# Second norm taken half by half of the tokens, in a one-core two-layer decoder step

## The reference, cut to what matters

```python
h = rmsnorm(x, norm_w) * (1 + scale) + shift      # scale, shift, gate from the condition
y = (mixer(h @ w_in) * silu(z)) @ w_out
x = x + gate * y
```

## Time and profile before

| what | before |
|---|---|
| median of three runs | 1167.5 us |
| profiled execution, its own time | 1165.51 us |
| its span | 1163.8 us |
| TensorE matmuls busy | 1124.7 us (97%) |
| VectorE busy | 627.2 us (54%) |
| ScalarE busy | 506.7 us (44%) |
| GpSimd busy | 150.7 us (13%) |
| mean granted TensorE clock | 0.989 |

### The profile page before, as it was taken

One profiled execution on the slowest core, in us unless ns is written; L12 is line 12 of the kernel. 1 busy time (PEld: TensorE's weight loads), 2 busy tenths in 40 slices (PEclk: granted clock), 3 DMA queues, 4 the chain that ended last, 5 costly groups with the idle time before them and its releaser, 6 DMA issues.

```text
span 1163.8 us, 25951 instructions
## 1 busy us (share of the span) xinstructions
PE 1124.7 (97%) x11029; PEld 1050.7 (90%) x11029; DVE 627.2 (54%) x1241; ACT 506.7 (44%) x1026; POOL 150.7 (13%) x156
## 2 busy tenths in 40 slices
PE   8999999999999999989998999999999999999998
PEld 6898988988898889869997999999999999998997
DVE  4766575667566666674333743453365336436432
ACT  4643344444444444453112544554365255447121
POOL 1000000101010101000000450162035005400000
PEclk9999999999999999989999999999999999999999
DMA  9863525352535343516233437432832562252531
GB/s 325 280 181 112 160 64 167 95 168 83 151 109 158 103 150 110 156 55 189 73 88 121 113 101 152 120 87 81 197 86 82 121 168 62 76 140 67 173 100 54
DMA packets 232153, 147.71 MB, mean 127 GB/s; under 512 B 7811, under 2 KB 226141, under 8 KB 231526
## 3 DMA queue, kind: packets, MB, share of 16 engines
q1 hardware_dynamic: 217392, 134.17, 40.3%
q10 hardware_dynamic: 14646, 11.89, 3.0%
HBM read 124.00 MB, written 22.02 MB: 125 GB/s over the span
## 4 chain that ended last, share of the span: by engine, by line
PE 86%; DVE 6%; issue 2%; ACT 2%; DMA 2%; SPq 1%; DVEq 0%; ACTq 0%
PE PJ L380 25%; PE PJ L1556 17%; PE PJ L1271 14%; PE PJ L401 7%; PE X L1153 1%; PE X L1249 1%; PE X L1672 1%; PE X L1167 1%; PE PJ L1581 1%; PE PJ L427 1%; PE X L1637 1%; PE X L1699 1%; PE PJ L624 1%; PE X L1120 1%; PE X L1251 1%
## 5 line engine op out<-in xcount | busy, mean ns | idle before, releaser
L353 DVE TENSOR_TENSOR w_lo<-raw,w_hi 128x1024 fp32r<-128x1024 f32 (+1 forms) x128 | 156.8, 1238 | 173.1 <-ACT w_hi L345 172.4
L345 ACT ACTIVATE w_hi<-raw 128x1024 fp32r<-128x1024 f32 (+1 forms) x128 | 129.1, 1024 | 156.8 <-PE PJ L1556 73.1
L1556 PE MATMUL PJ<-w_hi,h_hi 128*128 128x256 f32 x600 | 167.5, 287 | 0.8 <-DVE w_lo L353 0.7
L1556 PE MATMUL PJ<-w_lo,h_hi 128*128 128x256 f32 x600 | 164.6, 283 | 0.0
L380 PE MATMUL PJ<-h_hi,w_hi 128*128 128x288 f32 (+1 forms) x736 | 161.5, 301 | 0.2 <-ACT v_ L870 0.2
L380 PE MATMUL PJ<-h_hi,w_lo 128*128 128x288 f32 (+1 forms) x736 | 157.7, 296 | 0.0
L380 PE MATMUL PJ<-h_lo,w_hi 128*128 128x288 f32 (+1 forms) x736 | 157.3, 295 | 0.0
L1556 PE MATMUL PJ<-w_hi,h_lo 128*128 128x256 f32 x480 | 135.8, 283 | 0.0
L380 PEld LDWEIGHTS PJ<-h_hi,w_hi 128*128 128x128 f32 x736 | 118.1, 189 | 4.7 <-issue 3.8
L380 PEld LDWEIGHTS PJ<-h_hi,w_lo 128*128 128x128 f32 x736 | 118.9, 189 | 0.0
L380 PEld LDWEIGHTS PJ<-h_lo,w_hi 128*128 128x128 f32 x736 | 118.8, 189 | 0.0
(11 more groups left out here) (323 smaller groups left out, 2176.3 us busy)
## 6 DMA issues: line engine op xcount, KB each, us to landing
raw<-in_a_w_in_dram SPq DMA_DIRECT2D x48, 512.0 KB, 4.1
raw<-in_ada_w_dram SPq DMA_DIRECT2D x32, 512.0 KB, 3.7
raw<-in_b_w_in_dram SPq DMA_DIRECT2D x64, 256.0 KB, 3.4
kvc<-in_cache_kv_w_dram SPq DMA_DIRECT2D x24, 512.0 KB, 5.9
pre<-in_ada_w_dram SPq DMA_DIRECT2D x16, 512.0 KB, 10.0
s<-in_state_hgrn_dram SPq DMA_DIRECT2D x8, 1024.0 KB, 6.7
out_hgrn_sample_dram<-s ACTq DMA_DIRECT2D x8, 1024.0 KB, 5.0
raw<-in_a_w_out_dram SPq DMA_DIRECT2D x16, 512.0 KB, 5.1
```

Source lines behind the costliest of these rows:

```text
L345: act.activation(w_hi[:, i % SPLITS, 0:size], raw[:, n % RAWS, 0:size], ACT.Copy).then_inc(hi_done, 1)
L353: dve.tensor_tensor(w_lo[:, i % SPLITS, 0:size], raw[:, n % RAWS, 0:size], w_hi[:, i % SPLITS, 0:size].bitcast(F32), ALU.subtract).then_in ...
L1556: last = pe.matmul(PJ[:, tile // 2, tile % 2 * 256:tile % 2 * 256 + 256], a, b[:, k, :], start=(first and k == 0 and i == 0), stop=(kk == ...
```

## The change

**TensorE.** Output block 7 is made in two passes instead of one (`pe_out_halves`). Pass e takes, of every four consecutive tokens, the two with r = 2e and 2e+1: 288 tokens per matmul, read from the operand in strided pairs, and written side by side in one PSUM bank. Each pass walks all 16 input blocks. `norm_pe` of block 6 stands between the passes; block 7's sum of squares is made by halves, the first within pass 1, the second within the first attention rows.

**The norm.** All of it is done for the prompt tokens of half 0 (256 of them) and then of half 1. The squares are now written in turned order, by two ScalarE instructions per block. The samples go with half 1, and their four VectorE instructions or parts of such are now on GpSimd (`second_norm_seqs`).

**The first rows.** Tiles 0 and 1 are made for all feature blocks, then tiles 2 and 3.

```diff
 def norm_pe(sq, k):
-            for e in range(2):
-                last = pe.matmul(X[:, e, 0:HT], ones[:], sq[:, k % 2, e * HT:(e + 1) * HT],
-                                 start=(k == 0), stop=(k == KD - 1))
+            for e, (n0, n1) in enumerate(((0, HP), (HP, T))):
+                last = pe.matmul(X[:, e, 0:n1 - n0], ones[:], sq[:, k % 2, n0:n1], start=(k == 0), stop=False)
...
+        def norm_pe_last(sq, e):
+            pe.wait_ge(n_sq, 2 * KD + e)
+            n0, n1 = ((0, HP), (HP, T))[e]
+            pe.matmul(X[:, e, 0:n1 - n0], ones[:], sq[:, (KD - 1) % 2, n0:n1], start=False, stop=True).then_inc(n_ms, 1)
 def norm_square(xT, sq, k):
-            act.activation(sq[:, k % 2, :], xT[:, k, :], ACT.Square).then_inc(n_sq, 1)
+            act.activation(quarters(sq[:, k % 2, 0:TP]), perm(xT[:, k, 0:TP]), ACT.Square)
+            act.activation(sq[:, k % 2, TP:T], xT[:, k, TP:T], ACT.Square).then_inc(n_sq, 1)
 def second_norm_act(act, chain):
+            def inverse_root(e):
+                n0, n1 = ((0, HP), (HP, T))[e]
+                act.wait_ge(n_ms, 5 + KD + e)
+                chain(act.activation(rn1[:, n0:n1], X[:, e, 0:n1 - n0], ACT.Ln, bias=eps[:, 0:1], scale=1.0 / D))
+                act.activation(rnp[:, n0:n1], rn1[:, n0:n1], ACT.Exp, scale=-0.5).then_inc(n_r, 1)
...
+            last_square(0)
+            inverse_root(0)
+            act.wait_ge(out_half, 2)
+            hi(0, 0, 2)
+            split_hi(("a", 0, 1))
+            hi(0, 2, 5)
+            last_square(1)
+            hi(0, 5, KD)
+            inverse_root(1)
+            hi(1, 0, 5)
+            act.wait_ge(n_hs, 4)
+            act.activation(h_hi[:, :, TP:T], xa[:, :, TP:T], ACT.Copy).then_inc(n_hs, 1)
+            hi(1, 5, KD)
             split_hi(("a", 0, 2))
+        def second_norm_dve(dve, chain):
...
+            residual_half(chain, 0)
+            amplify_half(0)
             dve.wait_ge(n_xs, KD)
             dve.wait_ge(n_r, 2)
+            scale_x(0, 0)
             for k in range(1, KD):
+                scale_x(0, k)
+                low(0, k - 1)
                 if k == 2:
                     split_lo(("a", 0, 1))
+                if k == 4:
+                    residual_half(chain, 1)
+                    amplify_half(1)
+            dve.wait_ge(n_xs, KD + 1)
+            dve.wait_ge(n_r, 3)
+            scale_x(1, 0)
+            low(0, KD - 1)
+            for k in range(1, KD):
+                scale_x(1, k)
+                low(1, k - 1)
+            low(1, KD - 1)
             split_lo(("a", 0, 2))
+        def second_norm_seqs(pool):
+            xs = xa[:, :, TP:T]
+            pool.wait_ge(n_xs, KD + 1)
+            pool.wait_ge(n_r, 3)
+            nc.gpsimd.tensor_tensor(xs, xs, rnp[:, TP:T].unsqueeze(1).to_broadcast([P, KD, TS]), ALU.mult).then_inc(n_hs, 1)
+            pool.wait_ge(n_hs, 3)
...
+            nc.gpsimd.tensor_tensor(by_seq, by_seq, ada[:, 1, 0:KD, 1:].unsqueeze(3).to_broadcast([P, KD, DB, DS]),
+                                    ALU.add).then_inc(n_hs, 1)
+            pool.wait_ge(n_hs, 5)
+            for low_seqs in (h_hi[:, :, T:T + TS], h_lo[:, :, TP:T]):
+                nc.gpsimd.tensor_tensor(low_seqs, xs, h_hi[:, :, TP:T].bitcast(F32), ALU.subtract).then_inc(n_hs, 1)
+        def pe_out_halves(pe):
+            m = KD - 1
+            t = begin(OUT0 + m)
+            for e in range(2):
+                for n in range(16):
+                    if n % 8 == 0:
+                        pe.wait_ge(raw_split, split_no[("out0", m, n // 8)][0] + 1)
+                    wh, wl = parts_of(("out0", m, n // 8))
+                    for i, (a, b) in enumerate(((wh, o_hi(n)), (wh, oz_low[:, n, :]), (wl, o_hi(n)))):
+                        last = pe.matmul(PJ[:, 2 * t + e, 0:HT].rearrange("p (a r) -> p a r", r=2), a[:, n % 8, :],
+                                         b.rearrange("p (a r) -> p a r", r=4)[:, :, 2 * e:2 * e + 2],
+                                         start=(n == 0 and i == 0), stop=(n == 15 and i == 2))
+                    if n == 15 if e == 0 else 7 <= n < 15:
+                        last.then_inc(out_half, 1)
+                    if e == 1 and n == 4:
+                        norm_pe_last(nsq1, 0)
+                if e == 0:
+                    norm_pe(nsq1, m - 1)
+            last.then_inc(pj_ready, 1)
 def pe_first_rows(pe):
+            for e in range(2):
+                for k in range(KD):
+                    if e == 0 and k % 4 == 0:
+                        pe.wait_ge(raw_split, split_no[("a", 0, k // 4)][0] + 1)
+                    if e == 1 and k == 0:
+                        wait_read(pe, OUT0 + KD - 1)
+                    pe.wait_ge(n_hx, KD * (1 + e) + k + 1)
+                    pe.wait_ge(n_lo, KD * (1 + e) + k + 1)
+                    for tile in (2 * e, 2 * e + 1):
+                        last = product(PJ[:, tile, 0:256], tile, k)
+                    if e == 0 and k == 4:
+                        norm_pe_last(nsq1, 1)
+                last.then_inc((tiles_ready, pj_ready)[e], 1)
+            pe.wait_ge(n_hs, 6)
```

More of the change, by code:

```diff
@@ L218, in program @@
         n_hx = sem("n_hx")
+        out_half, x_half = sem("out_half"), sem("x_half")
         par_in, par_t, par_done = sem("par_in"), sem("par_t"), sem("par_done")
@@ L518, in amplify @@
             dve = nc.vector
-            seqs = lambda ap: ap.rearrange("p (b t) -> p b t", b=DB)
             wait_read(dve, OUT0 + m)
             dve.tensor_scalar(quarters(xa[:, m, 0:TP]), perm(xT1[:, m, 0:TP]), amp[:, m, 0:1], None, ALU.mult)
[L522 to L533, removed]
+            amplify_seqs(m)
@@ new lines, in amplify_seqs, with amplify_half @@
+        def amplify_seqs(m):
+            seqs = lambda ap: ap.rearrange("p (b t) -> p b t", b=DB)
+            nc.vector.tensor_tensor(seqs(xa[:, m, TP:T]), seqs(xT1[:, m, TP:T]),
+                                    amp[:, m, 1:].unsqueeze(2).to_broadcast([P, DB, DS]), ALU.mult).then_inc(n_xs, 1)
+        def amplify_half(e):
+            dve, m, r = nc.vector, KD - 1, slice(2 * e, 2 * e + 2)
+            if e == 0:
+                dve.wait_ge(x_half, 1)
+            else:
+                wait_read(dve, OUT0 + m)
+            ins = dve.tensor_scalar(quarters(xa[:, m, 0:TP])[:, r], perm(xT1[:, m, 0:TP])[:, r], amp[:, m, 0:1], None, ALU.mult)
+            if e == 0:
+                ins.then_inc(n_xs, 1)
+            else:
+                amplify_seqs(m)
@@ new lines, in residual_half @@
+        def residual_half(chain, e):
+            dve, m = nc.vector, KD - 1
+            s = m % 2
+            if e == 0:
+                dve.wait_ge(out_half, 1)
+            else:
+                dve.wait_ge(pj_ready, OUT0 + m + 1)
+            fours = lambda ap: ap.rearrange("p (a r) -> p a r", r=4)[:, :, 2 * e:2 * e + 2]
+            y = PJ[:, 2 * s + e, 0:HT].rearrange("p (a r) -> p a r", r=2)
+            x = fours(xT1[:, m, 0:TP])
+            dve.scalar_tensor_tensor(out=x, in0=y[:, 0:P], scalar=ada[:, 0, 2 * KD + m, 0:1], in1=x,
+                                     op0=ALU.mult, op1=ALU.add).then_inc(x_half, 1)
+            by_seq = lambda ap: ap.rearrange("p (b a) r -> p b a r", b=DB)
+            chain(dve.tensor_tensor(by_seq(fours(yg[:, s])), by_seq(y[:, P:]),
+                                    ada[:, 0, 2 * KD + m, 1:].unsqueeze(2).unsqueeze(3).to_broadcast([P, DB, 2, 2]), ALU.mult))
+            if e:
+                dve.tensor_tensor(xT1[:, m, TP:T], xT1[:, m, TP:T], yg[:, s], ALU.add).then_inc(pj_read[s], 1)
@@ new lines, in second_norm_dve, with scale_x, low @@
+        def second_norm_dve(dve, chain):
+            def scale_x(e, k):
+                c = slice(HP * e, HP * e + HP)
+                dve.tensor_tensor(xa[:, k, c], xa[:, k, c], rnp[:, c], ALU.mult).then_inc(n_xr, 1)
+            def low(e, k):
+                c = slice(HP * e, HP * e + HP)
+                dve.wait_ge(n_hx, KD * (1 + e) + k + 1)
+                if e == 0 and k < KD - 1:
+                    dve.wait_ge(out_half, 3 + k)
+                dve.scalar_tensor_tensor(out=h_lo[:, k, c], in0=xa[:, k, c], scalar=ada[:, 1, k, 0:1],
+                                         in1=h_hi[:, k, c].bitcast(F32), op0=ALU.add, op1=ALU.subtract).then_inc(n_lo, 1)
+            residual_half(chain, 0)
+            amplify_half(0)
@@ L2508, in _ @@
                     split_lo(("a", 0, 0))
-                dve_residual(dve, chain, 0, OUT0 + m, m, xT1, yg)
-                amplify(m)
+                if m < KD - 1:
+                    dve_residual(dve, chain, 0, OUT0 + m, m, xT1, yg)
+                    amplify(m)
                 if m == 3:
                     attention_tables(dve, chain)
-            second_norm_dve(dve)
+            second_norm_dve(dve, chain)
             attention_masks(dve)
@@ L2540, in _ @@
             pe.wait_ge(ada_done, 4 + AH)
-            for m in range(1, KD):
+            for m in range(1, KD - 1):
                 pe_out(pe, "out0", m, range(16))
```

(2 more changed lines are left out.)

74 lines of the change are left out of this document (31 added, 43 removed).

## The result

| what | before | after |
|---|---|---|
| median of five runs | 1166.64 us | 1174.74 us |
| lowest and highest | 1165.81 to 1167.86 | 1171.14 to 1176.68 |
| profiled execution, its own time | 1165.51 us | 1174.44 us |
| its span | 1163.8 us | 1172.8 us |
| TensorE matmuls busy | 1124.7 us (97%) | 1136.8 us (97%) |

The ratio is 1.0064, with a 95% interval of 1.0051 to 1.0077: slower by 7.5 us (8.1 us between the medians), and outside the range of the prediction. Note the two rows that an engineer would look at first. TensorE's share and its mean clock have hardly moved, and both look healthy. What the table hides is that TensorE's busy time got 12.1 us longer for the same multiplications.

A forecast was written before the change was run, and what follows sets the result against it. TensorE, busy 97%, was taken as the bound, with VectorE taking the path after the change. Pass 0, its wait and the rest, 6.4 + 0.9 + 31.1 = 38.4 us against 38.7, gave a median of 1167.2 us, range 1163.0 to 1170.5.

The forecast's parts named there:

- The step that failed: Block 7's two passes: strided-pair matmuls cost nothing extra, 6.4 us for 48; the other end was 6.4 more per pass.
- the sum of 38.4: Forecast from block 7's start to TensorE's second weight piece: 6.4 + 0.9 + 31.1 us, against 38.7 before.
- the stretch: From the norm matmuls' end ahead of block 7 to TensorE's start on the next head group's second weight piece, 38.70 us before.
- Rival C: Block 7's passes: TensorE reads pairs at half the rate, 10.1 us more together, 1177.3 us; chance 0.12.
- the first inverse root: Half 0's norm on ScalarE: done at E+4.4 us, E being the end of pass 0; logarithm and exponential about 0.5 each.
- rival B: Half 1 of the norm: GpSimd costs VectorE nothing, 4.4 us come back, 1162.8 us; chance 0.24.
- Pass 0 and its wait: Block 7's first pass: 6.4 us of matmuls plus a 0.9 us wait for a low part of the output weights.
- forecast A: The main forecast: TensorE's gap and slow clock go, VectorE takes the path, 0.3 us faster, 1167.2 us; chance 0.50.
- VectorE's pitches: VectorE in half 0 of the norm: 0.34 us per scale_x and 0.40 per low part.
- GpSimd against VectorE: Half 1 of the norm: each of four GpSimd instructions costs VectorE 1.1 us, 4.4 in all.
- The waits: First attention rows: TensorE idle 1.2 us at block 4 and 0.8 at block 7; VectorE idle 1.2 for the second root.
- Rival D: First attention rows: TensorE's clock falls to its lower level, 1168.4 to 1170.4 us; chance 0.14.

The follow-up runs named there:

- the last two kernels: Changed kernel with halves stored apart, samples' work on VectorE and a high part earlier; the second also has half 1's residual, square, sum earlier: 1163.05 and 1164.26 us.
- The later kernel with all edits: Changed kernel with halves stored apart, samples' work on VectorE, a high part earlier, and half 1's residual, square, sum and inverse root earlier: 1164.26 us, ratio 0.9961.

## Why the prediction was wrong, point by point

**The step that failed** is the price of a pair matmul: "Both ends: no cost, or as much again", of which I took none, since "pairs are nearer to in order than the turned reads are, and VectorE pays nothing even for those". The runs gave the other end, 0.256 against 0.133, 5.9 us for 48. Against the sum of 38.4 the stretch is 9.0 longer: pass 0 took 12.27 for 7.3, 5.0 more, and from its end to TensorE's start on the second piece it was 35.11 for 31.1, 4.0 more, as the half norm and the second residual stand behind the slow matmuls. The rows chosen were of other engines. VectorE's free turned reads the earlier trace rows said nothing of TensorE. ScalarE's price for a turned read, in the same group of rows, happened to point the right way, but it too was a row of another engine. The rule of the Trainium skill (SBUF — State Buffer, "SBUF cachelines") spoke for no cost: two accesses to a 16-byte line were to be enough. For TensorE's operand here they were not; pairs, with two accesses per line, ran as slow as every second element, and only whole lines were fast. Where the Trainium skill and the measurement differ, the measurement decides.

**Rival C** was the mechanism, with its place and its price. It gave a stretch of 38.4 + 10.1 = 48.5 us, and 47.38 was measured. Each pass took 0.5 less than C had it, since 0.256 is a little less than twice 0.133. Its wait in pass 0 did vanish: at the slow pace the low part of the piece was in time. VectorE's idle time ahead of the residual of half 1 was 1.45 us, not 4.6. The difference lies in work that also came later, which C had not moved: the first inverse root, behind 15 slow matmuls, 1.8 us, and the 1.35 us that the first low part then waited for pass 1. From the end of pass 1 to TensorE's start on the second piece is 21.45 us, and the forecast had 21.5 from the residual to there. C had a chance of 0.12. With an unknown whose two ends were no cost and twice the price, and no row of TensorE to choose by, that was too little, and the range left it out. (At its other end the range began at 1163.0, above rival B's own 1162.8.)

**Pass 0 and its wait** in forecast A: 7.3 us, measured 7.21 where the columns are in order. Removing the wait gave 1.06.

**The first inverse root** at E+4.4: with columns in order it is 0.97 + 2.00 + 0.43 in the chain and two ScalarE steps; after, the sum of squares ended at 638.31 and the root at 639.28, 0.97 later. Both parts are as forecast, at their pace.

**VectorE's pitches** 0.34 and 0.40: starts of 655.03, 655.43 and the next show 0.40 and 0.33. Right.

**GpSimd against VectorE**: 4.4 forecast, 3.9 measured, and rival B (no cost) falls. One row of layer 0 was enough to price this, because it was a row of the same two engines and the same kind of operands.

**The waits**: TensorE's were forecast as 1.2 at block 4 and 0.8 at block 7. With the columns in order they were 1.15 and 1.73. After, block 4 had none, as pass 1 ended so late, and block 7 had 1.72. The forecast did not count that the low part that block 7 waits for is the first VectorE instruction beside GpSimd, 1.0 us slower. VectorE's wait for the second root was forecast as 1.2 and measured as 1.35 in order and 1.61 after. In the 21.45 us these 0.4 more and GpSimd's 0.5 less cancel, which is luck.

**The rest of A** holds. In order the stretch is 37.82 where 38.4 was forecast, and the median is 0.8 us below the kernel before. The change without its strides is what A said: no difference that can be measured.

**Rival D**, the clock. It did fall, behind TensorE's wait of 1.72 us at block 7; the forecast had held against D that no gap would be over 1.3. The stages of after (columns as in the earlier trace rows):

```profile
650.00:655.00 5.00, 3.25 (x23) 2.71 (x22) 3.39 (x5) 2.02 (x4) 2.66 (x2) 1.00 1.01 339
655.00:660.00 5.00, 4.35 (x24) 4.38 (x25) 4.96 (x12) 3.46 (x7) 1.56 (x2) 0.66 0.77 215
```

After a stretch in which TensorE was busy 3.25 of 5 us, it had 0.66 in the next. But in that next one VectorE was busy 4.96 of 5, and it is VectorE that is on the chain, so the dip cost nothing that can be seen: the run with fours at column 2 had 1.00 from 650 to 670 us, and its stretch is 47.36 us. In the last two kernels all of 640 to 660 us was at 1.00, where the kernel before had 0.50 for 5 us.

## What to carry to other kernels

Price a new access pattern by a row of the engine that reads it, not of a neighbour; where no such row exists, give both ends real chances. If TensorE's moving operand (the one streamed against the loaded weights) of 4-byte elements is to be read in part, lay it out so that whole aligned groups of four are read, and let the engine that writes it do the striding. Here work given to GpSimd was not taken off VectorE, where instructions of both read two tensors of SBUF at the same time: four of 512 columns cost VectorE 3.9 us to save it 2.4.

## What the runs showed of the hardware that was not expected

- TensorE's moving operand showed two rates in six walks: 0.133 us per 288 columns of 4-byte elements when every aligned group of four is read whole (in order or every other group), and 0.256 to 0.261 for pairs, every second, one of four, and fours that begin at column 2.
- VectorE does not follow that rule: its half residual, which reads and writes x in strided pairs, took 0.48 us (L589), as its low parts in order did (L608). ScalarE's turned square took 1.11 us for 512 tokens (L508), near the 1.06 of the turned exponential and above the 0.63 of a copy in order. Whether ScalarE has the same two levels was not tried.
- The granted clock differs between executions of one kernel where TensorE picks up again after layer 0. The stages of the kernel with the halves stored apart, in the execution that was profiled:

```profile
510.00:530.00 20.00, 19.63 (x124) 14.52 (x123) 14.33 (x28) 7.52 (x13) 0.00 (x0) 0.85 0.18 61
530.00:620.00 90.00, 87.19 (x618) 85.90 (x617) 35.90 (x73) 21.84 (x28) 0.00 (x0) 0.96 0.38 115
```

  The kernel before had 0.98 and 1.00 there, and its block 7 began 7.7 us earlier in its execution. The later kernel with all edits had 0.95 and 1.00, and began block 7 at 620.19 with the same code up to there. So this, and not the code, makes most of that shift, and is one source of the spread of 5 to 8 us between runs of one kernel. The clearest pair is after and the run with fours at column 2, whose code is the same up to block 7, and whose block 7 began 3.42 us apart. The stage in which most of that arises, first for after:

```profile
540.00:560.00 20.00, 17.32 (x127) 16.87 (x126) 8.26 (x14) 6.28 (x8) 0.00 (x0) 1.00 0.59 167
```

  and then for fours at column 2:

```profile
540.00:560.00 20.00, 17.33 (x107) 16.89 (x106) 8.35 (x14) 6.29 (x8) 0.00 (x0) 0.83 0.52 140
```

  The same holds behind the stretch. From its end to the last instruction every profiled execution took either 506.2 us (before, in order, every other group of four, one of four, and the last two kernels) or 504.6 to 504.7 us (the other five), and those with 506.2 have a granted clock of 0.97 from 1040 to 1100 us, the others 1.00. Before, and then after:

```profile
1040.00:1100.00 60.00, 58.41 (x516) 55.85 (x515) 32.69 (x77) 30.56 (x68) 0.24 (x1) 0.97 0.36 108
...
1040.00:1100.00 60.00, 58.44 (x531) 55.14 (x530) 34.81 (x79) 31.79 (x69) 0.47 (x2) 1.00 0.51 135
```

  That is why the stretch, and not the time of one execution, is compared in the text. What decides the clock in an execution was not tried. Whether the strided gate in layer 0 costs something by itself also stays open: it was never run alone.
